# A fused two-block transformer kernel: where the squares of the recurrent heads' outputs are summed, and in what order VectorE gates and convolves

## Chip, cores and metric

The kernel runs on one core of one Trainium2 chip. The metric is the device time of one execution in microseconds (us); lower is better. The kernel before takes 2325.43 us, the median of three executions that lie between 2322.28 and 2327.88 us.

## The reference, cut to what matters

The reference is a diffusion-style block followed by a second block. The change touches only the second block's gated delta rule with eight heads of width 128 over 512 tokens, and there only what happens to its output `oa`:

```python
q = _l2norm(q) * 128 ** -0.5 ;  k = _l2norm(k)          # after a causal convolution of 4 taps and silu
for each chunk:   U = u_t - w @ S
                  o = q_dec @ S + p_intra @ U
                  S = S * exp(g_last) + k_dec.T @ U
oa = rmsnorm_2(oa, head_norm) * silu(za)                 # rmsnorm over the 128 columns of a head
y  = sigmoid(ga) * (oa @ w_a_out) + ...
```

`rmsnorm_2` needs, for each token and head, the sum of the squares of 128 values, then `1 / sqrt(sum / 128 + eps)`.

## The kernel before

The kernel is written engine by engine, with semaphores between the engines. Every large product is done three times over in single precision pieces: a weight block of 1 MB arrives in `raw`, ScalarE copies it to `w_hi` (line 742), GpSimd subtracts to get `w_lo` (line 670, four instructions for each block), and TensorE multiplies hi by hi, hi by lo and lo by hi (lines 2049 to 2051). These products keep TensorE busy nearly all the time.

The recurrent heads are worked in four pairs, `p` = 0 to 3, two heads (`a` = 0, 1) at a time. A pair needs four weight blocks (q, k, v, z). While TensorE does the small matrices of pair `p`, it fills its waits with pieces of the products for pair `p + 1` (`piece` and `fill`; a piece is six matmuls of 512 columns). 24 pieces, for q, k and v, go into the inversion levels and the four recurrence steps; the eight pieces of z stand behind them. The end of a pair, called the tail here, is this:

- ScalarE copies the output of each of the four steps `tt` from PSUM to `o_tok` (line 1164, 128x256). It then stores the v tiles of the next pair and splits a weight block (`pair_qkv(p + 1, 2)`, line 1176), waits for the sums, and takes the square root (line 1178).
- VectorE ends the convolutions 2 and 3 of the next pair (`convolve`, lines 1749 to 1756, four instructions for each), squares the whole of `o_tok` (line 1859), sums it (line 1860), waits for the root, inverts it (line 1862), scales `o_tok` in one instruction (line 1863), does convolution 4, then the two gatings (line 1869, `oaT`), then convolution 5.
- TensorE does pieces 0 to 3 of z, waits for the scaled `o_tok` (line 2616), transposes it (eight `turn`s, line 2158), does pieces 4 and 5, waits for the gated `oaT` (line 2624) and begins pair `p + 1`.
- The next pair begins with ScalarE's silu of convolutions 0 to 3, the squares of two of them (line 1117), silu of 4 and 5, then the roots (line 776). TensorE sums the squares with one-column matmuls (`sum_of`, line 2131), and between the first sums it has pieces 6 and 7 of z. Then it spreads the inverted roots over the partitions (`spread`, line 2152). The order is: sum 0, piece 6, sum 1, piece 7, spread 0, sum 2, spread 1, sum 3, spread 2, spread 3. ScalarE's queue puts the root of sum 0 behind silu 5, and silu 5 waits for convolution 5. Each spread is followed by a normalisation on VectorE, and behind the last ones come the transposes of k and v and the small products of the next pair, with no large product in between until `fill(3)` (line 2546).

In the last pair (`p` = 3) there is no next pair: TensorE does a whole gate block of sixteen pieces ahead of line 2616, and VectorE has no convolutions.

ScalarE's functions lie in tables; the program has a table load wherever the next function is not in the one that is loaded.

Of the kernel before, what the change touches and what calls it, by code (L numbers as in the profile page):

```python
# [19 lines left out]
ACT = mybir.ActivationFunctionType  # L20
ALU = mybir.AluOpType
AX = mybir.AxisListType


P = 128
# [3 lines left out]
NT = S // P  # L29
# [65 lines left out]
def build(nc, t, out):  # L95
# [23 lines left out]
    one_eps = fixed("one_eps", [P, 8])  # L119
# [4 lines left out]
    o_stat = fixed("o_stat", [P, 3, 8])  # L124
    sq2 = fixed("sq2", [P, 2, S])
    acc = fixed("acc", [P, S])
    tmp2 = fixed("tmp2", [P, 2, S])
# [107 lines left out]
    o_tok = r.over("o_tok", [P, 2, NT, P], decay_at)  # L235
# [53 lines left out]
    ps = nc.alloc_psum_tensor("ps", [P, 8, 512], F32)  # L289
# [12 lines left out]
    def over_width(m, w=P):  # L302

        return m.unsqueeze(2).broadcast_to([m.shape[0], m.shape[1], w])
# [123 lines left out]
    lat_std kr_mm kr_copied kr_put qk_scaled v_scaled qk_summed qk_squared qk_turned qk_stored qk_std at_turned at_exp  # L428
    at_copied at_out_hi fm_mm fm_hi_done y_t_done y_hi_done rsq_done g_hi_done gate_dve gate_act c_pad c_conv
    o_done c_silued c_sq Gb_mm Gb_exp d_diff d_exp nL_turned nLT_done lv_m1 lv_copied uw_mm uw_copied r_su r_oc  # L430
    o_sq o_std oa_hi_done m_tr m_T_done s_hi_done x_last y_turned dve_chain n_inv n_bc n_lo vec_tr tr_done
    ada_mod lat_gained lat_inv qk_mm qk_normed scl2_done at_scores at_prob at_out_lo fc_mm fc_half fc_split fz_done fm_lo_done
    y_lo_done g_lo_done ab_turned gate_cum c_normed kv_turned k_scaled qd_done kk_mm nL_done inv0_done lv_mm
    lv_done r_o r_ws r_u r_st o_scaled o_turned oa_lo_done rb_done gate_silu gate_scaled s_lo_done""".split()
    sem = {n: nc.alloc_semaphore(n) for n in names}
# [121 lines left out]
    with nc.Block() as block:  # L557
# [171 lines left out]
        def _(act):  # L729
# [118 lines left out]
            for j in range(2):  # L848
# [8 lines left out]
                                 scale=1.0 / KV_LORA).then_inc(sem["lat_std"], 1)  # L857
# [241 lines left out]
            for p in range(4):  # L1099
                u = first[f"pair{p}"]  # L1100
                if p == 0:
                    act.wait_ge(sem["c_pad"], 1)
                    pair_qkv(p, 0)
                    act.wait_ge(sem["gate_dve"], 3)
                    nc.scalar.activation(gp[:, 10, :, :], gp[:, 5, :, :], ACT.Exp)
                    nc.scalar.activation(gp[:, 8, :, :], gp[:, 9, :, :], ACT.Exp).then_inc(sem["gate_act"], 1)
                    pair_qkv(p, 1)
                    pair_qkv(p, 2)

                def silu(j):  # L1110
                    act.wait_ge(sem["c_conv"], 6 * p + j + 1)
                    nc.scalar.activation(conv[:, j, :], conv[:, j, :], ACT.Silu).then_inc(sem["c_silued"], 1)

                def square(j):
                    act.wait_ge(sem["c_silued"], 6 * p + j + 1)
                    act.wait_ge(sem["n_sum"], 4 + 4 * p + j - 1)
                    nc.scalar.activation(sq2[:, j % 2, :], conv[:, j, :], ACT.Square).then_inc(sem["c_sq"], 1)

                for j in range(4):
                    silu(j)  # L1120
                square(0)
                square(1)
                silu(4)
                silu(5)
                std_of(4 + 4 * p, 1.0)
                square(2)
                std_of(5 + 4 * p, 1.0)
                square(3)
                std_of(6 + 4 * p, 1.0)
                std_of(7 + 4 * p, 1.0)  # L1130
                for a in range(2):
                    if p:
                        act.wait_ge(sem["o_done"], 2 * p)
                    store_tile(u + 3, a, z_s[:, a, :], ACT.Silu)
                next_hi()
                for a in range(2):
                    h = 2 * p + a
                    act.wait_ge(sem["Gb_mm"], h + 1)
                    nc.scalar.activation(eGb[:, a, :], ps[:, 4 + a, :], ACT.Exp).then_inc(sem["Gb_exp"], 1)
                    act.wait_ge(sem["d_diff"], h + 1)  # L1140
                    nc.scalar.activation(decay[:, a, :, :], decay[:, a, :, :], ACT.Exp, scale=-1.0).then_inc(sem["d_exp"], 1)
                for a in range(2):
                    for i, dst in enumerate((nLT, prT)):
                        act.wait_ge(sem["nL_turned"], 4 * p + 2 * a + i + 1)
                        nc.scalar.activation(dst[:, a, :, :].rearrange("p t c -> p (t c)"), ps[:, (6 if i == 0 else 4) + a, :],
                                             ACT.Copy).then_inc(sem["nLT_done"], 1)
                for s in range(1, LEVELS):
                    for a in range(2):
                        n = (p * (LEVELS - 1) + s - 1) * 2 + a
                        act.wait_ge(sem["lv_m1"], n + 1)  # L1150
                        nc.scalar.activation(prod[:, a, :, :].rearrange("p t c -> p (t c)"), ps[:, 6 + a, :],  # L1151
                                             ACT.Copy).then_inc(sem["lv_copied"], 1)
                for a in range(2):
                    for i, dst in enumerate((u0[:, a, :, :].rearrange("p t c -> p (t c)"), wT[:, a, :])):
                        act.wait_ge(sem["uw_mm"], 4 * p + 2 * a + i + 1)
                        nc.scalar.activation(dst, ps[:, 4 + 2 * i + a, :], ACT.Copy).then_inc(sem["uw_copied"], 1)
                if p < 3:
                    pair_qkv(p + 1, 0)
                else:
                    gate_a(0)  # L1160
                    next_hi()
                for tt in range(NT):
                    act.wait_ge(sem["r_o"], 4 * p + tt + 1)
                    nc.scalar.activation(o_tok[:, :, tt, :], ps[:, 5 + 2 * (tt % 2), 0:2 * P].rearrange("p (a c) -> p a c", a=2),
                                         ACT.Copy).then_inc(sem["r_oc"], 1)
                    if tt == 1 and p < 3:
                        pair_qkv(p + 1, 1)
                    elif tt == 2 and p == 3:
                        gate_a(1)
                        next_hi()  # L1170
                    elif p == 3 and tt in (0, 1):
                        act.wait_ge(sem["o_done"], 6)
                        for k in range(3 * tt, 3 * tt + 3):
                            nc.scalar.activation(oa_hi[:, k, :], oaT[:, k, :], ACT.Copy).then_inc(sem["oa_hi_done"], 1)
                if p < 3:
                    pair_qkv(p + 1, 2)
                act.wait_ge(sem["o_sq"], p + 1)
                nc.scalar.activation(o_stat[:, 1, :], o_stat[:, 0, :], ACT.Sqrt, bias=one_eps[:, 0:1],
                                     scale=1.0 / P).then_inc(sem["o_std"], 1)


            for k in range(6, HA):
# [159 lines left out]
        def _(dve):  # L1342
            chain = [0]

            def link(ins):

                ins.then_inc(sem["dve_chain"], 1)
                chain[0] += 1
                dve.wait_ge(sem["dve_chain"], chain[0])

            V = nc.vector
# [87 lines left out]
            for i in range(2):  # L1439
                ins = V.scalar_tensor_tensor(scl[:, i, :], mod[:, 8:16, i], 1.0,  # L1440
                                             vecT[:, VEC_AT["norm1_g"]:VEC_AT["norm1_g"] + KT], ALU.add, ALU.mult)
# [173 lines left out]
            for j in range(4):  # L1615
                u, v, o = first["gf"] + j, merged("ga", j), merged("wfa", j)
                for jj in range(2):
                    dve.wait_ge(bank_stored[bank_of(u, jj)], stored_count(u, jj))
                    dve.wait_ge(sem["tile_done"], tile_count(o, jj))
                    p = bank(o, jj)  # L1620
# [4 lines left out]
                for jj in range(2):  # L1625
# [3 lines left out]
                    p = bank(o, 2 + jj)  # L1629
# [129 lines left out]
            def convolve(p, j):  # L1759
                convolve_a(p, j)  # L1760
                convolve_b(p, j)

            for p in range(4):
# [89 lines left out]
                    convolve(p + 1, 2)  # L1853
                    convolve(p + 1, 3)

                dve.wait_ge(sem["r_oc"], 4 * p + 4)
                flat = o_tok[:, :, :, :].rearrange("p a t c -> p (a t) c")
                sq = tmp2[:, :, :].rearrange("p a (t c) -> p (a t) c", c=P)
                link(V.tensor_tensor(sq, flat, flat, ALU.mult))
                V.tensor_reduce(o_stat[:, 0, :], sq, AX.X, ALU.add).then_inc(sem["o_sq"], 1)  # L1860
                dve.wait_ge(sem["o_std"], p + 1)
                link(V.reciprocal(o_stat[:, 2, :], o_stat[:, 1, :]))
                V.tensor_tensor(flat, flat, over_width(o_stat[:, 2, :]), ALU.mult).then_inc(sem["o_scaled"], 1)
                if p < 3:
                    convolve(p + 1, 4)
                for a in range(2):
                    dve.wait_ge(sem["o_turned"], 2 * p + a + 1)
                    dve.wait_ge(bank_stored[bank_of(u + 3, a)], stored_count(u + 3, a))
                    V.scalar_tensor_tensor(oaT[:, 2 * p + a, :], ps[:, 4 + a, :], col("head_norm_2"), z_s[:, a, :],
                                           ALU.mult, ALU.mult).then_inc(sem["o_done"], 1)  # L1870
                if p < 3:
                    convolve(p + 1, 5)

            for k in range(HA):
# [4 lines left out]
            for j in range(4):  # L1879
                u, v = gated("aout", "sig", j), gated("aout", "proj", j)  # L1880
                for jj in range(2):
                    dve.wait_ge(bank_stored[bank_of(u, jj)], stored_count(u, jj))
                    dve.wait_ge(sem["tile_done"], tile_count(v, jj))
                    p = bank(v, jj)
# [158 lines left out]
        def _(pe):  # L2043
# [448 lines left out]
            for p in range(4):  # L2492
# [120 lines left out]
                        piece(first[f"pair{p + 1}"] + 3, k)  # L2613
                else:
                    wide_gemm(gated("aout", "sig", 2), h_hi, h_lo)
                pe.wait_ge(sem["o_scaled"], p + 1)
                for a in range(2):
                    for tt in range(NT):
                        ins = turn(ps[:, 4 + a, tok(tt)], o_tok[:, a, tt, :])
                    ins.then_inc(sem["o_turned"], 1)  # L2620
# [224 lines left out]
```

## Time and profile before

| | before |
|---|---|
| median of three executions | 2325.43 us |
| the profiled execution | 2328.51 us |
| its span, first to last instruction | 2326.6 us |
| TensorE matmul busy | 2240.3 us (96%) |
| VectorE busy | 893.2 us (38%) |
| ScalarE busy | 830.4 us (36%) |
| GpSimd busy | 882.5 us (38%) |
| mean granted TensorE clock | 0.982 of full |

Times inside the span are microseconds from its start. A row of a timeline shows the start, the time that the merged instructions cover, the engine, the line, what is written and read, the count, and in brackets the time that the engine had been idle and what ended that. The three tails of pairs 0, 1 and 2 begin their transposes at 1015, 1124 and 1237 us, the tail of pair 3 at 1344 us. Matmuls overlap each other, so their durations add up to more than the time they take.

### The profile page before, as it was taken

To read this page: it belongs to the slowest core of one execution; us is meant where nothing else is said; L and a number is where in the kernel's file an instruction comes from. 1 tells how busy PE (TensorE), PEld (TensorE's weight loads), DVE (VectorE), ACT (ScalarE), POOL (GpSimd) and SP (SyncE) were. 2 spreads that over 40 slices of the span, in tenths; PEclk is the share of its full clock that TensorE was granted. 3 is DMA by queue.
4 is the path that set the end of the run, shared out by engine and by line. 5 is a ranking of instruction groups with operands and counts; after the bars stand their busy time and mean duration, and the time that the engine had idled before them with its cause. 6 is when DMAs were issued, how large, how long until landed. Compare 5 with 4: busy or idle time off the path is not lost.

```text
span 2326.6 us, 29170 instructions
## 1 busy us (share of the span) xinstructions
PE 2240.3 (96%) x11780; PEld 1862.3 (80%) x11780; DVE 893.2 (38%) x1411; ACT 830.4 (36%) x1208; POOL 882.5 (38%) x640
## 2 busy tenths in 40 slices
PE   6999999989999989989999999999999999999998
PEld 3767778878888868979797988888888988888887
DVE  2456855441211246474747320414143344222102
ACT  2455533232322335242424322535333443322212
POOL 0325953434444434030212144222254524444442
PEclk9989999999999999999999999999999999999998
DMA  6411333522233233020201022121232412322321
GB/s 229 149 54 55 127 102 103 169 73 91 91 96 102 91 110 96 19 73 9 101 19 55 19 91 92 54 94 52 100 118 91 135 50 90 107 90 94 104 90 55
DMA packets 179970, 205.93 MB, mean 89 GB/s; under 512 B 3364, under 2 KB 170768, under 8 KB 179472
## 3 DMA queue, kind: packets, MB, share of 16 engines
q1 hardware_dynamic: 176912, 195.17, 25.9%
q10 hardware_dynamic: 2944, 9.15, 1.1%
q8 instruction: 82, 1.34, 0.2%
q14 instruction: 32, 0.26, 0.0%
HBM read 198.01 MB, written 6.29 MB: 88 GB/s over the span
## 4 chain that ended last, share of the span: by engine, by line
PE 83%; DVE 6%; ACT 2%; POOL 2%; issue 1%; DMA 1%; ACTq 0%; DVEq 0%; SPq 0%
PE ps L2049 20%; PE ps L2051 20%; PE ps L2050 19%; PE ps L2158 3%; PE ps L2574 2%; PE ps L2565 2%; PE ps L2370 2%; POOL w_lo L670 2%; PE ps L2643 2%; PE ps L2572 2%; PE ps L2660 1%; PE ps L2152 1%; PE ps L2336 1%; PE ps L2096 1%; PE ps L2098 1%; PE ps L2097 1%
## 5 line engine op out<-in xcount | busy, mean ns | idle before, releaser
L670 POOL TENSOR_TENSOR w_lo<-raw,w_hi 128x512 fp32r<-128x512 f32 x586 | 780.3, 1363 | 1378.5 <-ACT w_hi L742 1378.5
L2049 PE MATMUL ps<-h_hi,w_hi 128*128 128x512 f32 x1384 | 560.4, 405 | 12.9 <-DVE h_lo L1389 4.2
L2051 PE MATMUL ps<-h_hi,w_lo 128*128 128x512 f32 x1384 | 544.3, 393 | 0.0
L2050 PE MATMUL ps<-h_lo,w_hi 128*128 128x512 f32 x1384 | 543.3, 393 | 0.0
L742 ACT ACTIVATE w_hi<-raw 128x2048 fp32r<-128x2048 f32 x150 | 285.7, 1905 | 373.5 <-PE ps L2051 365.7
L2049 PEld LDWEIGHTS ps<-h_hi,w_hi 128*128 128x128 f32 x1384 | 262.7, 190 | 74.1 <-issue 10.7
L2051 PEld LDWEIGHTS ps<-h_hi,w_lo 128*128 128x128 f32 x1384 | 262.4, 190 | 57.0
L2050 PEld LDWEIGHTS ps<-h_lo,w_hi 128*128 128x128 f32 x1384 | 263.0, 190 | 52.6 <-issue 1.5
L2049 PE MATMUL ps<-g_hi,w_hi 128*128 128x512 f32 x256 | 101.0, 394 | 0.0
L2051 PE MATMUL ps<-g_hi,w_lo 128*128 128x512 f32 x256 | 100.4, 392 | 0.0
L2050 PE MATMUL ps<-g_lo,w_hi 128*128 128x512 f32 x256 | 99.4, 388 | 0.0
L1656 DVE SCALAR_TENSOR_TENSOR xT<-ps,mod,xT 128x512 f32<-128x512 f32 x40 | 30.0, 751 | 167.2 <-PE ps L2051 167.1
L1900 DVE SCALAR_TENSOR_TENSOR score_b<-ps,xT 128x128 f32<-128x128 f32 (+3 forms) x64 | 31.3, 490 | 152.0 <-PE ps L2643 145.6
L1151 ACT ACTIVATE prod<-ps 128x512 f32<-128x512 f32 x48 | 28.7, 598 | 129.6 <-PE ps L2565 129.6
L1693 DVE TENSOR_TENSOR rsq<-relu 128x512 f32<-128x512 f32 x32 | 22.2, 693 | 133.1 <-ACT relu L761 133.1
L2049 PE MATMUL ps<-s_hi,w_hi 128*128 (+1 forms) x176 | 69.4, 394 | 1.0 <-issue 1.0
L2051 PE MATMUL ps<-s_hi,w_lo 128*128 (+1 forms) x176 | 69.0, 392 | 0.0
L2050 PE MATMUL ps<-s_lo,w_hi 128*128 (+1 forms) x176 | 68.3, 388 | 0.0
L1830 DVE COPY_PREDICATED inv<-masks,ps 128x512 f32<-128x512 uint32 x40 | 29.2, 730 | 83.2 <-PE ps L2574 83.2
L761 ACT ACTIVATE relu<-ps 128x512 f32<-128x512 f32 x32 | 19.1, 598 | 108.3 <-PE ps L2051 102.6
L2051 PEld LDWEIGHTS ps<-g_hi,w_lo 128*128 128x128 f32 x256 | 48.1, 188 | 11.3
L2050 PEld LDWEIGHTS ps<-g_lo,w_hi 128*128 128x128 f32 x256 | 48.1, 188 | 10.7
(414 smaller groups left out, 3939.5 us busy)
## 6 DMA issues: line engine op xcount, KB each, us to landing
raw<-w_in SPq DMA_DIRECT2D x48, 1024.0 KB, 5.2
raw<-w_down SPq DMA_DIRECT2D x27, 1024.0 KB, 5.1
raw<-ada_w SPq DMA_DIRECT2D x24, 1024.0 KB, 5.2
raw<-w_gate_up SPq DMA_DIRECT2D x22, 1024.0 KB, 5.1
raw<-w_up SPq DMA_DIRECT2D x16, 1024.0 KB, 5.4
raw<-w_mkv SPq DMA_DIRECT2D x8, 1024.0 KB, 5.5
raw<-w_out SPq DMA_DIRECT2D x4, 1024.0 KB, 5.5
xT<-bias_band SPq DMA_DIRECT2D x2, 2048.0 KB, 9.9
```

The lines of the kernel that those rows point to most:

```text
L670: ins = nc.gpsimd.tensor_tensor(w_lo[:, split_at[u] % 2, cols], raw[:, u % 2, cols], w_hi[:, split_at[u] % 2, cols].bitcast(F32), ALU.subt ...
L742: nc.scalar.activation(w_hi[:, split_at[u] % 2, 0:n], raw[:, u % 2, 0:n], ACT.Copy).then_inc(sem["w_hi_done"], 1)
L1900: V.scalar_tensor_tensor(score_b[:, n % 3, 0:nk], ps[:, 2 + n % 2, 0:nk], -(DB ** -0.5), xT[:, hh, S - nk:S], ALU.mult, ALU.subtract).then ...
L2049: T.matmul(out_, wh, hi, start=start, stop=False, skip_group_check=True)
L2050: T.matmul(out_, wh, lo, start=False, stop=False, skip_group_check=True)
L2051: return T.matmul(out_, wl, hi, start=False, stop=stop, skip_group_check=True)
L2158: return T.transpose(out_, src, const[0:rows, CONST_AT["ident"]:CONST_AT["ident"] + rows])
L2370: ins = T.matmul(ps[(h % 2) * 64:(h % 2 + 1) * 64, out_bank(n), tok], v[:, kt, (h % 8) * 64:(h % 8 + 1) * 64], pT[:, n % 2, kt * P:(kt + 1 ...
L2565: ins = T.matmul(ps[:, 6 + a, tok(tt)], nLT[:, a, tt, :], inv[:, a, tt, :], start=True, stop=True)
L2572: T.matmul(ps[:, 4 + a, tok(tt)], invT[:, a, tt, :], prod[:, a, tt, :], start=True, stop=True)
L2574: ins = T.matmul(ps[:, 6 + a, tok(tt)], prod[:, a, tt, :], invT[:, a, tt, :], start=True, stop=True)
L2643: T.matmul(ps[:, 2 + n % 2, 0:nk], query[:, tok(q)], kbT[:, hh // 2, 0:nk], start=True, stop=True).then_inc(sem["b_scores"], 1)
```

## The change

The two large instructions of VectorE that square and sum `o_tok` go. Instead ScalarE, right after each of its copies out of PSUM, runs two `Square` activations over the same PSUM values (128x128 each, one for each head) and has each leave its row sum in a column of `o_stat`. The root is taken at once behind the fourth step, ahead of the stores and the split in `pair_qkv(p + 1, 2)`. VectorE scales `o_tok` in two halves, one for each head, with a count of the semaphore for each, and TensorE waits for each half by itself. VectorE's gatings move in front of convolution 4, so that both convolutions 4 and 5 stand behind them.

```diff
@@ ScalarE
                 for tt in range(NT):
                     act.wait_ge(sem["r_o"], 4 * p + tt + 1)
-                    nc.scalar.activation(o_tok[:, :, tt, :], ps[:, 5 + 2 * (tt % 2), 0:2 * P].rearrange("p (a c) -> p a c", a=2),
-                                         ACT.Copy).then_inc(sem["r_oc"], 1)
+                    out_of = ps[:, 5 + 2 * (tt % 2), 0:2 * P].rearrange("p (a c) -> p a c", a=2)
+                    nc.scalar.activation(o_tok[:, :, tt, :], out_of, ACT.Copy)
+                    for a in range(2):
+                        ins = nc.scalar.activation(tmp2[:, a, tt * P:(tt + 1) * P], out_of[:, a, :], ACT.Square,
+                                                   accum_out=o_stat[:, 0, a * NT + tt:a * NT + tt + 1])
+                    ins.then_inc(sem["r_oc"], 1)
...
+                act.wait_ge(sem["r_oc"], 4 * p + 4)
+                nc.scalar.activation(o_stat[:, 1, :], o_stat[:, 0, :], ACT.Sqrt, bias=one_eps[:, 0:1],
+                                     scale=1.0 / P).then_inc(sem["o_std"], 1)
                 if p < 3:
                     pair_qkv(p + 1, 2)
-                act.wait_ge(sem["o_sq"], p + 1)
-                nc.scalar.activation(o_stat[:, 1, :], o_stat[:, 0, :], ACT.Sqrt, bias=one_eps[:, 0:1],
-                                     scale=1.0 / P).then_inc(sem["o_std"], 1)
@@ VectorE
-                dve.wait_ge(sem["r_oc"], 4 * p + 4)
-                flat = o_tok[:, :, :, :].rearrange("p a t c -> p (a t) c")
-                sq = tmp2[:, :, :].rearrange("p a (t c) -> p (a t) c", c=P)
-                link(V.tensor_tensor(sq, flat, flat, ALU.mult))
-                V.tensor_reduce(o_stat[:, 0, :], sq, AX.X, ALU.add).then_inc(sem["o_sq"], 1)
                 dve.wait_ge(sem["o_std"], p + 1)
                 link(V.reciprocal(o_stat[:, 2, :], o_stat[:, 1, :]))
-                V.tensor_tensor(flat, flat, over_width(o_stat[:, 2, :]), ALU.mult).then_inc(sem["o_scaled"], 1)
-                if p < 3:
-                    convolve(p + 1, 4)
+                for a in range(2):
+                    V.tensor_tensor(o_tok[:, a, :, :], o_tok[:, a, :, :], over_width(o_stat[:, 2, a * NT:(a + 1) * NT]),
+                                    ALU.mult).then_inc(sem["o_scaled"], 1)
                 for a in range(2):
                     dve.wait_ge(sem["o_turned"], 2 * p + a + 1)
                     dve.wait_ge(bank_stored[bank_of(u + 3, a)], stored_count(u + 3, a))
                     V.scalar_tensor_tensor(oaT[:, 2 * p + a, :], ps[:, 4 + a, :], col("head_norm_2"), z_s[:, a, :],
                                            ALU.mult, ALU.mult).then_inc(sem["o_done"], 1)
                 if p < 3:
+                    convolve(p + 1, 4)
                     convolve(p + 1, 5)
@@ TensorE
-                pe.wait_ge(sem["o_scaled"], p + 1)
                 for a in range(2):
+                    pe.wait_ge(sem["o_scaled"], 2 * p + a + 1)
                     for tt in range(NT):
                         ins = turn(ps[:, 4 + a, tok(tt)], o_tok[:, a, tt, :])
                     ins.then_inc(sem["o_turned"], 1)
```

The semaphore `o_sq` goes with them.

## Rows read from the trace of the kernel before

**Rows 1.** The page's chain that ended last, shares of the span by engine.
```profile
PE 83%; DVE 6%; ACT 2%; POOL 2%; issue 1%; DMA 1%; ACTq 0%; DVEq 0%; SPq 0%
```
**Rows 2.** Who waited for whom, first tail (1012 to 1035): total, times, longest.
```profile
PE ps L2131 <- DVE oaT L1869: 2.2, 1, 2.2
...
PE ps L2158 <- DVE o_tok L1863: 1.5, 1, 1.5
```
**Rows 3.** Table by stretch: length, TensorE busy (matmuls), granted clock, DMA share, GB/s.
```profile
1015.00:1021.00 6.00, 3.84 (x20) 1.00 0.35 105
...
1132.00:1136.00 4.00, 4.00 (x15) 0.50 0.00 0
...
1248.00:1252.00 4.00, 4.00 (x14) 0.50 0.00 0
```
**Rows 4.** Timeline of TensorE, tails of pairs 0, 1 and 2.
```profile
1015.12 1.09 PE L2158 MATMUL ps<-const,o_tok 128*128 128x128 f32 x8 [1.49 <-DVE o_tok L1863]
...
1021.15 1.05 PE L2131 MATMUL ps<-const,sq 128*128 128x1 f32 x8 [2.19 <-DVE oaT L1869]
...
1026.44 1.13 PE L2152 MATMUL ps<-const,stat 128*128 128x128 f32 x8 [0.49 <-DVE stat L1369]
...
1123.88 1.09 PE L2158 MATMUL ps<-const,o_tok 128*128 128x128 f32 x8 [1.49 <-DVE o_tok L1863]
...
1129.91 1.75 PE L2131 MATMUL ps<-const,sq 128*128 128x1 f32 x8 [2.19 <-DVE oaT L1869]
...
1138.50 1.91 PE L2152 MATMUL ps<-const,stat 128*128 128x128 f32 x8
...
1236.75 1.09 PE L2158 MATMUL ps<-const,o_tok 128*128 128x128 f32 x8 [1.49 <-DVE o_tok L1863]
```
**Rows 5.** Timeline of VectorE in the first tail.
```profile
1010.37 1.22 DVE L1859 TENSOR_TENSOR tmp<-o_tok 128x1024 f32<-128x1024 f32 x1
...
1013.45 1.61 DVE L1863 TENSOR_TENSOR o_tok<-o_tok,o_stat 128x1024 f32<-128x1024 f32 x1
1014.98 1.50 DVE L1749 TENSOR_SCALAR conv<-pad_in,vecT 128x512 f32<-128x512 f32 x1
1016.51 1.68 DVE L1750 SCALAR_TENSOR_TENSOR conv<-pad_in,vecT,conv 128x512 f32<-128x512 f32 x1
...
1019.69 1.40 DVE L1869 SCALAR_TENSOR_TENSOR oaT<-ps,vecT,z_s 128x512 f32<-128x512 f32 x2
...
1023.09 0.75 DVE L1756 SCALAR_TENSOR_TENSOR conv<-pad_in,vecT,conv 128x512 f32<-128x512 f32 x1
```
**Rows 6.** Timeline of ScalarE in the first tail.
```profile
1008.17 0.39 ACT L1164 ACTIVATE o_tok<-ps 128x256 f32<-128x256 f32 x1 [6.50 <-PE ps L2608]
...
1009.41 1.93 ACT L742 ACTIVATE w_hi<-raw 128x2048 fp32r<-128x2048 f32 x1
...
1013.20 1.28 ACT L1112 ACT_TABLE_LOAD   x1
1014.49 2.20 ACT L1112 ACTIVATE conv<-conv 128x512 f32<-128x512 f32 x4
1016.59 1.14 ACT L1117 ACTIVATE sq<-conv 128x512 f32<-128x512 f32 x2
```
**Rows 7.** ScalarE's groups by shape, whole span: busy us, mean ns of one.
```profile
L1221 ACT ACTIVATION_READ_ACCUMULATOR prob_b<-score_b,b_min 128x1 f32 x64 | 12.3, 192 | 0.0
...
L1229 ACT ACTIVATE probT_b<-ps 128x128 f32<-128x128 f32 x16 | 4.4, 277 | 19.5 <-PE ps L2158 19.5
```
**Rows 8.** Timeline of GpSimd in the first tail.
```profile
1011.42 6.23 POOL L670 TENSOR_TENSOR w_lo<-raw,w_hi 128x512 fp32r<-128x512 f32 x4 [8.08 <-ACT w_hi L742]
```
**Rows 9.** Timeline of VectorE in the last pair's tail.
```profile
1338.50 1.62 DVE L1863 TENSOR_TENSOR o_tok<-o_tok,o_stat 128x1024 f32<-128x1024 f32 x1
```
**Rows 10.** Timeline of TensorE in the last pair's tail.
```profile
1343.95 1.03 PE L2158 MATMUL ps<-const,o_tok 128*128 128x128 f32 x8
```
**Rows 11.** Table by stretch around 311 us, columns as in rows 3.
```profile
311.00:316.00 5.00, 5.00 (x40) 0.83 0.69 209
```

More of the change, by code:

```diff
@@ L430, in build @@
     o_done c_silued c_sq Gb_mm Gb_exp d_diff d_exp nL_turned nLT_done lv_m1 lv_copied uw_mm uw_copied r_su r_oc
-    o_sq o_std oa_hi_done m_tr m_T_done s_hi_done x_last y_turned dve_chain n_inv n_bc n_lo vec_tr tr_done
+    o_std oa_hi_done m_tr m_T_done s_hi_done x_last y_turned dve_chain n_inv n_bc n_lo vec_tr tr_done
     ada_mod lat_gained lat_inv qk_mm qk_normed scl2_done at_scores at_prob at_out_lo fc_mm fc_half fc_split fz_done fm_lo_done
```

## The prediction

> **What bounds the kernel now.** I read the page's chain first: 83% of it is TensorE [rows 1]. So VectorE's or ScalarE's time counts only where TensorE waits for it. Then the waits of one tail: TensorE waits 1.5 us for the scaled `o_tok` and 2.2 us for `oaT` [rows 2]. Last the granted clock by stretch: 1.00 in the first tail, and 0.50, the 1.2 GHz level, in the other two [rows 3], behind the same two waits [rows 4]. The timelines then give the order of work. All times below are in the first tail's own time; the other tails are the same, shifted by 108.8 and 221.6 us.
>
> TensorE's idle times in the first tail: 1.49 ahead of the transposes at 1015.12, 2.19 ahead of sum 0 at 1021.15, 0.49 ahead of spread 0 at 1026.44, together 4.17 us [rows 4]. The fallen clock is dearer. From 1123.88 to 1236.75 are 112.87 us, from 1015.12 to 1123.88 are 108.76 [rows 4]: the fall behind the second tail costs 4.11 us, and one more fall stands behind the third. The profiled execution has two, 8.2 us. Without them its 2328.51 us would be 2320.3. It lies 3.1 us above the median 2325.43, about the price of one fall less.
>
> **VectorE's part.** The squares and sums took 2.5 us ahead of the root (start 1010.37) [rows 5]. They go. What VectorE waits for now is ScalarE: the fourth copy starts at 1008.17 and takes 0.39 [rows 6]. Two Squares with an accumulator read each are added. No row has a Square of that shape with a sum; the nearest are the 128x128 copy out of PSUM at 0.277 and the accumulator read at 0.192 [rows 7]. Overlapped completely a pair costs ScalarE 0.55, one behind the other 0.94; I take 0.75, nearer the middle. Root: table load 1.28 (the length that a load has in rows 6), root 0.30, so it is there at 8.56 + 0.75 + 1.6 = 1010.9 (10.7 to 11.1). The inversion adds 0.25. Half a scaling is no row; half of 1.61 is 0.81, half of the plain 1.22 is 0.61 [rows 5]. I take 0.75. Both halves are ready at about 1012.7. TensorE's four pieces end at 15.12 - 1.49 = 1013.6 [rows 4]. The **first wait goes**, 1.5 us, and the two halves gain nothing more, because both are early.
>
> The earlier twelve pairs of Squares lie in waits of ScalarE, which was idle 6.50 us ahead of the fourth copy [rows 6]; they cost nothing. If one were late by its 0.75, the steps' fills would still cover it.
>
> The transposes now start at 1013.6. Gating a takes the half transposed, 0.6 later, and the pair of gatings takes 1.4 [rows 5]: 1014.2 to 1015.6. TensorE has pieces 4 and 5: from the transposes' start to their end it was 21.15 - 2.19 - 15.12 = 3.84 us [rows 4], so they end at 1017.45. The **second wait**, for `oaT`, **goes** too.
>
> **What is late next.** Sum 0 needs a square of a silu on ScalarE. Its queue: root till 1010.9, stores and split 2.9 (from the copy's end at 8.56, less the overlap, to the split's end at 11.34), load 1.28, four silus 2.1, one square 0.6: 1017.8. Sum 0 starts at 1017.9, 3.2 us earlier than now, after 0.4 us of waiting.
>
> From there TensorE has 26.44 - 0.49 - 21.15 = 4.80 us of work [rows 4], till 1022.7. Spread 0 hangs on something else: on convolution 5, through silu 5, a table load, the root and the inversion. That convolution ended at 1023.84 [rows 5], spread 0 began at 1026.44 [rows 4]: 2.60 us behind it. Where does it end now? Gatings till 1015.6, then both convolutions. One that nothing disturbs took 23.84 - 21.01 = 2.83 us [rows 5], counted from its first instruction, which overlaps the gatings by 0.08. But GpSimd's four subtractions follow the split. They began at 1011.42 and covered 6.23 us [rows 8]. Now the split stands behind the root and ends at 1013.8, so they run until about 1020. VectorE's instructions beside them are longer: the first two of convolution 4 took 1.50 and 1.68, while one of the second's kind alone takes 0.75, and convolution 4 took 19.69 - 14.98 = 4.71 [rows 5], 1.9 us more than 2.83, for two such instructions. Now it lies wholly beside GpSimd: three of its instructions would be caught, +2.8. Bounds: two caught, +1.9; four, +3.7. Convolution 5 ends at 15.6 + 2 x 2.83 + 2.8 = 1024.0 (23.1 to 24.9), against 1023.84. The 2.5 us saved on VectorE go into 1.5 us of waiting for the transposes and 0.9 us more beside GpSimd.
>
> So spread 0 starts at 1026.6 (25.7 to 27.5), where it started at 1026.44. **The sum without the clock** is nothing: +0.2 us a tail (-0.7 to +1.1). The idle time is 0.4 + 3.9 = 4.3, where it was 4.17. But it lies in one piece of 3.9 us (3.0 to 4.8) instead of pieces of 1.5, 2.2 and 0.5.
>
> **The last pair** has slack: its scaling began at 1338.50 and took 1.62 [rows 9], and the transposes came at 1343.95 [rows 10], 3.8 us later. ScalarE's steps there are about 0.75 later each, which the gate block covers. Zero; if that cover were gone, at most 1 us.
>
> **The clock.** It fell in two of three tails after idles of 1.49 and 2.19 with 3.84 us of pieces between [rows 3, 4]. It also fell at 311 to 316 us with TensorE never idle, in a run of one-column sums [rows 11]. Now the idle is 3.9 us, longer than any in these tails, with one-column sums around it. And behind it stand spreads and sums only, no pieces. I expect a fall in each of the three tails. A spread group took 1.91 at the low level against 1.13, a sum 1.75 against 1.05 [rows 4]. Four spreads and two sums on the path: 4 x 0.78 + 2 x 0.70 = 4.5. The first transposes behind them add some 0.7 (estimate, half a group of the 1.03 of rows 10 more). A fall costs 5.2 us. Low end 3.0, if it comes one spread and one sum late and has gone before the transposes; high end 8, if it lasts into the small products, where both engines take turns until `fill(3)`.
>
> The Trainium skill (TensorE: Matmul & The Clock Gate, section Why this matters for your kernels) asks that bursts of matmuls have no long idle gap between them, lest the clock fall. That speaks against joining the waits.
>
> The Trainium skill (ScalarE: Activation LUTs, section What ACT_TABLE_LOAD costs) adds 1.38 us of drain to each 1.28 us load. By that, two loads ahead of sum 0 would put it at 1020.7; its 4.80 us of work still end ahead of spread 0, and the sum stays. The row speaks against it: the load that starts at 1013.20 is followed by the silu at 1014.49 [rows 6].
>
> **How it adds up.** 2328.5 - 8.2 (two falls that the old waits caused) + 3 x 0.2 + 3 x 5.2 = 2336.5 us. Where convolution 4 meets only two subtractions it is 2.7 less. I forecast 2335.
>
> **Rivals.**
> - *The clock holds.* The stalls move and no fall comes: 2320.3 + 0.6 = 2321; with the shorter convolution 4, 2318. For it: the first tail had 4.2 us of idle and no fall. Against: never one piece of this length in a tail. It decides if convolution 5 ends so early that the idle ahead of spread 0 stays near the 2.19 that the first tail bore. The price is three falls of 5.2, 15.6 us. Chance 0.20.
> - *Some falls only, or cheap ones.* Two falls of 5.2, 2331, or three of 3.0, 2330, down to one, 2326. For it: one tail in three was spared before. Chance 0.22.
> - *The clock stays low until the next large product.* Mechanism: behind spread 0 come only short matmuls until `fill(3)`, and if these do not bring the clock back, all TensorE's steps in the chain stay doubled. 2321 + 3 x 8 = 2345. It decides if the transposes of k and v still run at the low level. Chance 0.08.
> - *The change does not do what it says*, by Square needing a table of its own: one load of 1.28 more in each pair, hidden in ScalarE's waits before the first step. It changes nothing and is within the above.
> - My forecast, three falls of about 5: 2329 to 2340, chance 0.50. It is the case that ends slower.
>
> **How the numbers follow.** 0.2% of the median is 4.7 us, about what a measurement of this kernel can tell from no change. Faster is below 2320.8: most of the first rival and a little more, 0.20. Slower is above 2330.1: the forecast but its lowest part, a quarter of the second rival, all of the third, 0.56. Same: 0.24. For eight in ten the range takes in both other sides: 2317 to 2343. That leaves out part of the third rival and the lowest ends. The forecast's own range is 2329 to 2340.
>
> **What would show it.** Right: no wait of TensorE for `o_tok` or `oaT` in the three tails; transposes some 13 us in front of spread 0 (11.3 now), one idle of 3 to 4.8 us ahead of spread 0; convolution 4 with three long instructions; clock 0.50 over the spreads of each tail; VectorE's busy time down by 4 x 2.5, less what GpSimd adds, ScalarE's up by 16 x 0.75 to 0.94. Wrong: an idle under 2.5 us ahead of spread 0 (the convolution's price was too high), a clock of 1.00 behind a long idle (then the time is near 2320), or a wait ahead of sum 0 of over 1.5 us (ScalarE's queue was mis-sized).

## The result and the profile after

The changed kernel takes 2332.03 us, the median of eight runs (2327.89 to 2338.45); the kernel before takes 2323.94 us beside it (eight runs, 2320.61 to 2327.88). The ratio is 1.0033, 95% interval 1.0023 to 1.0043: slower by a third of a percent. The profiled execution of the changed kernel took 2330.06 us, its span is 2328.3 us.

| | before | after |
|---|---|---|
| TensorE matmul busy, us | 2240.3 | 2243.0 |
| VectorE busy, us | 893.2 | 880.5 |
| ScalarE busy, us | 830.4 | 838.6 |
| mean granted clock | 0.982 | 0.981 |
| from the first tail's transposes to the second's | 108.76 | 114.40 |
| from the second's to the third's | 112.87 | 113.07 |

The chain is still TensorE's, 84% where it was 83% [rows 1]. Here is TensorE's timeline of the changed kernel in the first tail (start, time covered, line, count, and in brackets the idle time before and what ended it). The rest of such a tail are pieces of six matmuls.

```profile
1008.04 1.03 PE L2158 MATMUL ps<-const,o_tok 128*128 128x128 f32 x8
...
1012.17 1.02 PE L2131 MATMUL ps<-const,sq 128*128 128x1 f32 x8 [0.34 <-issue]
...
1014.53 0.95 PE L2131 MATMUL ps<-const,sq 128*128 128x1 f32 x8
...
1020.48 2.04 PE L2152 MATMUL ps<-const,stat 128*128 128x128 f32 x8 [3.49 <-DVE stat L1373]
1022.32 1.71 PE L2131 MATMUL ps<-const,sq 128*128 128x1 f32 x8
1023.88 2.05 PE L2152 MATMUL ps<-const,stat 128*128 128x128 f32 x8
1025.73 1.71 PE L2131 MATMUL ps<-const,sq 128*128 128x1 f32 x8
1027.30 3.76 PE L2152 MATMUL ps<-const,stat 128*128 128x128 f32 x16
1031.84 3.67 PE L2158 MATMUL ps<-const,conv 128*128 128x128 f32 x16 [0.78 <-DVE conv L1780]
```

Against rows 4: the transposes follow the pieces with no wait (1.49 us before), sum 0 waits 0.34 us (2.19 before), and spread 0 waits 3.49 us (0.49 before). From there on a spread group covers 2.04 us against 1.13 [rows 4]. The other two tails have the same three idle times within 0.03 us.

The same kernel's table by stretch (length, busy time and count of TensorE, weight loads, VectorE, ScalarE, GpSimd, then granted clock, DMA share, GB/s):

```profile
1012.00:1016.00 4.00, 3.83 (x25) 3.50 (x26) 3.89 (x5) 1.22 (x3) 1.79 (x2) 1.00 0.24 57
1016.00:1020.00 4.00, 0.99 (x5) 0.47 (x3) 1.81 (x3) 2.05 (x3) 0.00 (x0) 0.88 0.58 206
1020.00:1024.00 4.00, 3.52 (x17) 3.55 (x17) 1.04 (x3) 1.31 (x4) 0.00 (x0) 0.50 0.00 0
...
1032.00:1036.00 4.00, 4.00 (x20) 4.00 (x21) 2.56 (x5) 1.23 (x1) 3.99 (x4) 0.50 0.01 2
1136.00:1140.00 4.00, 4.00 (x21) 4.00 (x21) 0.87 (x2) 0.26 (x1) 0.00 (x0) 0.50 0.00 0
1248.00:1252.00 4.00, 4.00 (x19) 4.00 (x20) 1.05 (x3) 1.04 (x4) 0.00 (x0) 0.50 0.00 0
```

The clock falls around the end of the idle ahead of spread 0, in all three tails: in stretches of half a microsecond the fall begins 1.5 us ahead of spread 0 in the first tail, 0.2 us behind its start in the second and 0.2 us ahead of it in the third. Before, the first tail kept 1.00 and the others fell behind their second wait [rows 3]. VectorE's timeline of the changed kernel in the first tail, answering to rows 5:

```profile
1005.29 0.20 DVE L1861 RECIPROCAL o_stat<-o_stat 128x8 f32<-128x8 f32 x1 [0.27 <-ACT o_stat L1180]
1005.53 1.29 DVE L1863 TENSOR_TENSOR o_tok<-o_tok,o_stat 128x512 f32<-128x512 f32 x2
1008.68 1.41 DVE L1868 SCALAR_TENSOR_TENSOR oaT<-ps,vecT,z_s 128x512 f32<-128x512 f32 x2 [1.85 <-PE ps L2158]
1010.00 0.94 DVE L1753 TENSOR_SCALAR conv<-pad_in,vecT 128x512 f32<-128x512 f32 x1
1010.98 1.67 DVE L1754 SCALAR_TENSOR_TENSOR conv<-pad_in,vecT,conv 128x512 f32<-128x512 f32 x1
1012.68 1.66 DVE L1759 SCALAR_TENSOR_TENSOR conv<-pad_in,vecT,conv 128x512 f32<-128x512 f32 x1
...
1017.13 0.75 DVE L1760 SCALAR_TENSOR_TENSOR conv<-pad_in,vecT,conv 128x512 f32<-128x512 f32 x1
```

The scaling is ready 1.2 us ahead of the transposes, VectorE then waits 1.85 us for them, and three instructions of convolution 4 are long. GpSimd in the same stretch:

```profile
1008.12 5.67 POOL L670 TENSOR_TENSOR w_lo<-raw,w_hi 128x512 fp32r<-128x512 f32 x4 [9.77 <-ACT w_hi L742]
```

ScalarE's timeline shows what the Squares cost, which no row of before had:

```profile
1002.75 0.39 ACT L1165 ACTIVATE o_tok<-ps 128x256 f32<-128x256 f32 x1 [5.98 <-PE ps L2608]
1003.03 0.27 ACT L1167 ACTIVATE tmp<-ps 128x128 f32<-128x128 f32 x1
1003.18 0.21 ACT L1167 ACTIVATION_READ_ACCUMULATOR tmp<-ps 128x1 f32 x1
1003.28 0.28 ACT L1167 ACTIVATE tmp<-ps 128x128 f32<-128x128 f32 x1
1003.43 0.21 ACT L1167 ACTIVATION_READ_ACCUMULATOR tmp<-ps 128x1 f32 x1
1003.67 1.28 ACT L1180 ACT_TABLE_LOAD   x1
1004.96 0.30 ACT L1180 ACTIVATE o_stat<-o_stat,one_eps 128x8 f32<-128x8 f32 x1
```

A pair of Squares with their reads ends 0.50 us behind the copy's end (1003.64 against 1003.14).

The two profiled spans differ by only 1.7 us, though the three tails together lost 6.2 us (from the end of the first tail's pieces to the last pair's transposes 336.50 us, before 330.32). The rest was gained where nothing was changed: the first tail's pieces end 5.6 us earlier in the execution of after (1008.0 against 1013.6). Ahead of them the granted clock fell six times, and seven times in the execution of before, where several falls were also longer. A single execution is a draw of such falls, and medians are needed.

### The profile page after: what moved, and what is told of

Same layout as the page of the kernel before. It is cut to its first block, busy times and chain, and to the rows that moved or that the text cites. A ratio compares the mean times of both kernels' runs of the same rounds, so it can differ in the third digit from the quotient of the medians.

```text
span 2328.3 us, 29230 instructions
## 1 busy us (share of the span) xinstructions
PE 2243.0 (96%) x11780; PEld 1869.0 (80%) x11780; DVE 880.5 (38%) x1407; ACT 838.6 (36%) x1272; POOL 878.6 (38%) x640
## 4 chain that ended last, share of the span: by engine, by line
PE 84%; DVE 5%; ACT 2%; POOL 2%; issue 1%; DMA 1%; ACTq 0%; DVEq 0%; SPq 0%
PE ps L2049 20%; PE ps L2051 20%; PE ps L2050 20%; PE ps L2158 3%; PE ps L2574 2%; PE ps L2565 2%; PE ps L2370 2%; POOL w_lo L670 2%; PE ps L2643 2%; PE ps L2572 2%; PE ps L2152 1%; PE ps L2660 1%; PE ps L2336 1%; PE ps L2096 1%; PE ps L2098 1%
## 5 line engine op out<-in xcount | busy, mean ns | idle before, releaser
L2050 PEld LDWEIGHTS ps<-g_lo,w_hi 128*128 128x128 f32 x256 | 48.1, 188 | 10.7
```

The costliest lines, as they stand in the source:

```text
L2050: T.matmul(out_, wh, lo, start=False, stop=False, skip_group_check=True)
```

## The experiments

Theory A is that of the prediction: the steps themselves come out even, convolution 5 sets spread 0 and joins the idle times into one, and the clock falls there. The rivals are in the expectations. All experiments ran beside the kernel before; where the first four ran its median was 2325.38, where the last four ran 2324.00 us. So a time of one group and a time of the other can be told apart only to about 1.4 us. The ratios are as recorded; for the first four they lie about 0.001 above the quotient of the two medians given here.

**One edit of the order undone.** Convolution 4 stands ahead of the gatings again.

```diff
+                if p < 3:
+                    convolve(p + 1, 4)
                 for a in range(2):
                     dve.wait_ge(sem["o_turned"], 2 * p + a + 1)
...
                 if p < 3:
-                    convolve(p + 1, 4)
                     convolve(p + 1, 5)
```

> The changed kernel with one edit undone: convolution 4 stands again between the scaling and the gatings. Theory A (the long idle ahead of spread 0 lets the clock fall, and it comes from both convolutions standing behind the gatings, beside GpSimd): here convolution 4 runs from 1012.7 on, in the time in which VectorE now waits for the transposes, and partly ahead of GpSimd's subtractions; convolution 5 ends 1.5 to 2.5 us earlier in each tail than in the changed kernel, spread 0 comes at most 2.5 us after the last piece, few or no falls stand behind the three tails: 2312 to 2318 us, 0.6 to 0.9% under the changed kernel and faster than the kernel before. Rival B (ScalarE's Squares and reads are what costs): nothing changes, 2330 to 2334 us, and the clock falls as in the changed kernel.

Measured: 2325.78 us (2319.23 to 2332.19), ratio 1.0012, interval 1.0000 to 1.0025. Neither number of the expectations came: the kernel is no faster than the kernel before. TensorE in the three tails of that kernel:

```profile
1011.96 1.02 PE L2132 MATMUL ps<-const,sq 128*128 128x1 f32 x8 [0.35 <-DVE oaT L1870]
...
1018.82 1.88 PE L2153 MATMUL ps<-const,stat 128*128 128x128 f32 x8 [2.09 <-DVE stat L1373]
...
1130.80 1.28 PE L2153 MATMUL ps<-const,stat 128*128 128x128 f32 x8 [2.11 <-DVE stat L1373]
...
1242.84 1.13 PE L2153 MATMUL ps<-const,stat 128*128 128x128 f32 x8 [2.08 <-DVE stat L1373]
```

The steps behave as theory A has it: the idle ahead of spread 0 is 2.1 us, 1.4 less. But the clock still fell in all three tails of the profiled execution (0.50 over 1020 to 1028, 1132 to 1144 and 1248 to 1256 us). My belief that an idle of 2 us would be borne was wrong. Rival B is refuted too: the kernel is 6 us faster than the changed one with every Square in place.

**The other edit alone.** The kernel before, with the gatings ahead of both convolutions.

```diff
-                if p < 3:
-                    convolve(p + 1, 4)
                 for a in range(2):
                     dve.wait_ge(sem["o_turned"], 2 * p + a + 1)
...
                 if p < 3:
+                    convolve(p + 1, 4)
                     convolve(p + 1, 5)
```

> The kernel before with one edit of the change alone: VectorE's gatings in front of convolutions 4 and 5, everything else as before. Theory A: the first wait of 1.49 us stays, the second (2.19 us) goes, since the gatings end about 1.7 us ahead of TensorE's piece 5; the idle ahead of spread 0 grows from 0.49 to about 2.5 us, because convolution 5 ends where it did (1023.8 in the first tail's time). Falls in one to three of the tails: 2322 to 2334 us. Rival B (the Squares on ScalarE are what costs): no different from the kernel before or up to 2 us faster, whatever the idle ahead of spread 0.

Measured: 2326.09 us (2322.56 to 2334.23), ratio 1.0010, interval 0.9999 to 1.0021, inside theory A's range. Rival B's number (no different from the kernel before) is met as well, so this time alone does not tell them apart; the trace has the steps that theory A named. The idle ahead of spread 0 is 1.99 us, the second wait is gone. In the profiled execution the clock held in the first tail and fell in the other two. With the fall a tail's period is 113.05 us, without it 107.79, against 108.76 before. So this order saves 1.0 us in the steps and loses it in falls.

**The subtractions moved away.** The changed kernel, with the tail's split between silu 4 and silu 5 of the next pair.

```diff
-            def pair_qkv(p, kind):
+            def pair_qkv(p, kind, split=True):
...
                     store_tile(first[f"pair{p}"] + kind, a, pad_in[:, 2 * kind + a, 3:3 + S])
-                next_hi()
+                if split:
+                    next_hi()
...
                 silu(4)
+                if p:
+                    next_hi()
                 silu(5)
...
                 if p < 3:
-                    pair_qkv(p + 1, 2)
+                    pair_qkv(p + 1, 2, split=False)
```

> The changed kernel with one wait's cause moved: ScalarE's split of a weight block that follows the stores in the tail (and with it GpSimd's four subtractions) stands between silu 4 and silu 5 of the next pair instead, about 8 us later. Theory A: convolutions 4 and 5 have no subtraction beside them, take 2 x 2.83 instead of about 8, convolution 5 ends 2 to 2.8 us earlier, the idle ahead of spread 0 is 1 to 1.6 us instead of 3.5, the clock holds in all three tails: 2311 to 2316 us. Rival C (the convolutions' length does not matter, spread 0 waits for ScalarE's queue): the split delays silu 5 and the root by up to 1.9 us, spread 0 comes later than in the changed kernel, 2332 us or more.

Measured: 2315.78 us (2309.39 to 2324.6), ratio 0.9967, interval 0.9954 to 0.9980. The convolutions are now short, here VectorE in the first tail:

```profile
1011.68 0.48 DVE L1756 TENSOR_SCALAR conv<-pad_in,vecT 128x512 f32<-128x512 f32 x1
1012.19 0.75 DVE L1757 SCALAR_TENSOR_TENSOR conv<-pad_in,vecT,conv 128x512 f32<-128x512 f32 x1
1012.98 0.75 DVE L1762 SCALAR_TENSOR_TENSOR conv<-pad_in,vecT,conv 128x512 f32<-128x512 f32 x1
...
1016.52 0.75 DVE L1763 SCALAR_TENSOR_TENSOR conv<-pad_in,vecT,conv 128x512 f32<-128x512 f32 x1
```

Both take 5.59 us (from 1011.68 to 1017.27) instead of 7.88 in the changed kernel (from 1010.00 to 1017.88). That settles the price of the subtractions beside them: 2.3 us a tail. Rival C is refuted. The idle ahead of spread 0 is 1.86 us, more than the 1 to 1.6 us expected. In the profiled execution no tail had a fall. But that execution is the fastest of the twelve, 6.4 us under the median, and its mean granted clock is 0.989, while the median of the twelve is 0.985. So most of the others had falls that this trace does not show; whether they stood in these tails, no trace tells. That the time came out inside theory A's range is therefore no proof that the clock held.

**TensorE kept busy in the idle of the changed kernel.** Twelve matmuls that nobody reads stand behind piece 7.

```diff
+                def keep_busy(n):
+                    for _ in range(n):
+                        T.matmul(ps[:, 7, :], h_hi[:, 0, 0:P], h_hi[:, 0, :], start=True, stop=True)
...
                         piece(u + 3, 6 + j)
+                    if p and j == 1:
+                        keep_busy(12)
```

> The changed kernel with twelve matmuls of 512 columns added behind piece 7 in each of the three tails, into a bank of PSUM that nobody reads; they do no work of the reference and take about 2.7 us at the full clock, inside the idle of 3.5 us. Theory A (the loss is the clock, and the idle makes it fall): spread 0 starts no later than before, the clock stays at 1.00 over the spreads and transposes, each tail is 4 to 6 us shorter, 2315 to 2320 us. Rival D (the clock falls because of the spreads and one-column sums themselves, or the tail is longer for another reason): falls stay, 2330 to 2336 us.

Measured: 2314.15 us (2312.25 to 2319.89), ratio 0.9965, interval 0.9951 to 0.9979. This is 17.9 us under the changed kernel, with more work and nothing taken away, and 0.9 us below theory A's range. TensorE in its first tail, and the table by stretch:

```profile
1022.66 1.13 PE L2152 MATMUL ps<-const,stat 128*128 128x128 f32 x8 [0.83 <-DVE stat L1373]
...
1029.04 1.97 PE L2158 MATMUL ps<-const,conv 128*128 128x128 f32 x16 [0.78 <-DVE conv L1780]
```

```profile
1018.00:1022.00 4.00, 3.84 (x17) 2.83 (x16) 1.99 (x3) 1.88 (x2) 0.00 (x0) 1.00 0.63 220
1022.00:1026.00 4.00, 3.33 (x30) 3.37 (x31) 1.60 (x5) 1.75 (x6) 0.00 (x0) 1.00 0.00 0
```

Spread 0 comes 12.42 us behind the transposes (1022.66 - 1010.24), in the changed kernel 12.44. What differs is the clock and what follows at it: from spread 0 to the first matmul of `fill(3)` are 15.58, 15.23 and 15.23 us here, 21.39, 20.05 and 19.99 in the changed kernel. Rival D is refuted in these tails: spreads and sums alone did not bring the clock down.

**TensorE kept busy in the waits of the kernel before.**

```diff
+                if p < 3:
+                    keep_busy(6)
                 pe.wait_ge(sem["o_scaled"], p + 1)
...
+                    keep_busy(9)
                     pe.wait_ge(sem["o_done"], 2 * p + 2)
```

> The kernel before with matmuls of 512 columns added into the two waits of each of the three tails, six ahead of the wait for the scaled outputs and nine ahead of the wait for the gated ones, into a bank of PSUM that nobody reads; they do no work of the reference. Theory A (a fall of the clock stands behind the waits of some tails of the kernel before, two in the profiled execution): none is left there, each spared fall gives back 4 us: 2316 to 2322 us, under the kernel before by one to one and a half falls on the mean, with less spread. Rival (the falls behind these tails are not made by these waits): 2323 to 2328 us, as the kernel before.

Measured: 2315.61 us (2313.19 to 2320.42), ratio 0.9964, interval 0.9950 to 0.9977, 8.4 us under the kernel before, 0.4 us below theory A's range. Its periods are 108.78 us in both cases. So the kernel before loses 8.4 us to falls behind its old waits. At 4.1 us each that is two on the mean, not one to one and a half. Kept busy, before and after differ by 1.5 us (2315.61 and 2314.15, whose runs overlap). In the traces the changed kernel's two periods are shorter by 0.2 and 0.6 us (108.58 and 108.21 from transposes to transposes). So the change's steps come out about even.

**Both improvements together.** Convolution 4 ahead of the gatings as in the first experiment, and the late split of the third; the diffs are those two.

> The changed kernel with both edits of the first runs: convolution 4 in front of the gatings again, and ScalarE's split between silu 4 and silu 5. Theory A: convolution 4 runs in VectorE's wait for the transposes, nothing stands beside it on GpSimd, convolution 5 ends some 4.5 us earlier than in the changed kernel, spread 0 finds its root ready when piece 7 ends; no idle of over 0.5 us in a tail, no fall there: 2303 to 2309 us, 0.7 to 0.9% under the kernel before. Rival (the late split moves the wait to silu 5 and GpSimd's subtractions into the gatings or the normalisation): an idle of 1 us or more ahead of spread 0 or later, 2311 us or more, no better than the late split alone.

Measured: 2304.26 us (2300.69 to 2306.78), ratio 0.9915, interval 0.9898 to 0.9931, as theory A had it. TensorE in its first tail has no idle from the transposes to the ones of k and v:

```profile
1009.94 1.03 PE L2162 MATMUL ps<-const,o_tok 128*128 128x128 f32 x8
...
1013.56 0.95 PE L2135 MATMUL ps<-const,sq 128*128 128x1 f32 x8
...
1018.16 1.13 PE L2156 MATMUL ps<-const,stat 128*128 128x128 f32 x8
...
1024.54 1.97 PE L2162 MATMUL ps<-const,conv 128*128 128x128 f32 x16 [0.78 <-DVE conv L1783]
```

The 0.78 us ahead of the transposes of k and v, over the 0.5 us of theory A, are in all the kernels here. The root for spread 0 is inverted at 1018.02, as piece 7 ends, so the rival's wait there did not come. The periods are 104.38 and 104.02 us, 4.4 and 8.9 below the two of before. This kernel beats both, before and after.

**One scaling instead of two halves.**

```diff
-                for a in range(2):
-                    V.tensor_tensor(o_tok[:, a, :, :], o_tok[:, a, :, :], over_width(o_stat[:, 2, a * NT:(a + 1) * NT]),
-                                    ALU.mult).then_inc(sem["o_scaled"], 1)
+                flat = o_tok[:, :, :, :].rearrange("p a t c -> p (a t) c")
+                V.tensor_tensor(flat, flat, over_width(o_stat[:, 2, :]), ALU.mult).then_inc(sem["o_scaled"], 1)
```

> The changed kernel with the scaling done in one instruction and one count again, as in the kernel before; all else is the changed kernel. Theory A (the halves gain nothing, since the scaled outputs are ready about 1.2 us before TensorE's pieces end): within 2 us of the changed kernel, 2330 to 2334 us, the transposes start without a wait. Rival (the halves are what takes away the first wait): a wait of 0.3 us or more ahead of the transposes comes back.

Measured: 2333.13 us (2330.13 to 2336.81), ratio 1.0039, interval 1.0027 to 1.0052, 1.1 us from the changed kernel, with no wait ahead of the transposes. The halves gain nothing.

**The first experiment, kept busy.** Its kernel with `keep_busy(8)` behind piece 7.

> The changed kernel with convolution 4 in front of the gatings again, and eight matmuls of 512 columns behind piece 7 in each of the three tails, into a bank of PSUM that nobody reads; they do no work of the reference and take 1.8 us of the idle of 2.1 us. Theory A (that order gains 1.8 us a tail in the steps, and the falls behind an idle of 2.1 us took it back): no fall in the tails, 1.6 to 1.9 us a tail under the changed kernel that was kept busy: 2307 to 2312 us. Rival (the falls come for another reason): 2322 to 2328 us, as without these matmuls.

Measured: 2313.93 us (2309.07 to 2318.74), ratio 0.9956, interval 0.9943 to 0.9969. The falls in the tails are gone and with them 11.9 us against the kernel that was not kept busy. From sum 0 to sum 0 its tails are 107.17 and 106.81 us apart, against 108.58 and 108.21 in the changed kernel kept busy, so the steps are 1.4 us a tail shorter; from the first tail's transposes to the last pair's they are 4.2 us shorter (316.84 against 321.09). The medians do not show it: 0.2 us instead of 4.2, and above the 2307 to 2312 that theory A wanted. In the profiled execution the clock fell once more ahead of the first tail than in that of the changed kernel kept busy (at 136 to 148 us; both fell at about 916), and once more behind the tails (1628 to 1636). The other runs point the same way: the median of their mean granted clocks is 0.987, against 0.988 to 0.989 there, and among runs whose mean clock is 0.989 the three there took 2312.25 to 2313.97 us, the two here 2309.07 and 2310.35, 3.6 us less on the mean. So at an equal clock most of the gain is there, and further falls hide it; why this kernel has more of them, and where they lie in the other runs, stays open.

## Why the prediction was right, point by point

The forecast was 2335 us and slower, by three falls of the clock behind one long idle. It was 2332.03. The direction and the mechanism came as told. That the number lies within 3 us is in part luck. The sum stood on 2320.3 us for the kernel before without its two falls, taken from one profiled execution that lies 4.6 us above the median of the eight; kept busy, that kernel takes 2315.61, 4.7 us less. Against that, the new falls came out dearer (17.9 us by the medians instead of 15.6) and the steps cheaper (-1.5 instead of +0.6). The difference between the two kernels is the fairer test: the sum makes it -8.2 + 0.6 + 15.6 = 8.0 us, and it is 8.1.

To compare steps, 5.56 us are added to the times of after, so that the pieces end at 1013.6 in both.

- *Both waits go*: right. The root was ready at 1010.8 (forecast 1010.9), both halves at 1012.4 (1012.7), the gatings ran from 1014.2 to 1015.65 (1014.2 to 1015.6).
- *A pair of Squares costs 0.75 us*: too high, it is 0.50; ScalarE's busy time rose by 8.2 us, 0.51 for each pair, not 12 to 15. Of the 0.21 us of a read 0.12 lie inside its Square. It moved nothing, since the scaling was early anyway.
- *Sum 0 after 0.4 us of waiting at 1017.9*: 0.34 us, 1017.7.
- *Convolutions 4 and 5 take 8.4 us beside the subtractions*: 7.9. Three instructions were caught, as forecast, but the first by only 0.46 us. The late split measured this price by itself.
- *Spread 0 at 1026.6 behind one idle of 3.9 us*: 1026.0 and 3.5 us, inside the bounds.
- *The sum without the clock is nothing*: forecast +0.2 us a tail. The changed kernel kept busy is 1.5 us under the kernel before kept busy, so about -0.5 us a tail (-0.2 and -0.6 by the periods of the traces).
- *The old waits cost two falls, 8.2 us*: 8.4 by keeping the kernel before busy.
- *Three falls of 5.2 us*: in the traces 5.8, 4.8 and 4.8 us between spread 0 and `fill(3)`, mean 5.1; by the medians 17.9 us for the three, 6.0 each. What makes the medians' number the larger is not settled; a few falls elsewhere would do it, since the changed kernel's median lies 2.0 us above its profiled execution.
- *VectorE's busy time down by four times 2.5 us, less what GpSimd adds*: it fell by 12.7 us, more than forecast. The eight squares and sums of the kernel before had held 10.7; the rest was not followed up.
- *The 1.38 us of drain that go with a table load by the Trainium skill* (ScalarE: Activation LUTs, section What ACT_TABLE_LOAD costs): the measurement decides against it here. The read ahead of the load ends at 1003.64, the load runs from 1003.67 to 1004.95, and the root starts at 1004.96, so there is no room for it on either side.
- *The rule that bursts of matmuls should have no long idle between them* (the Trainium skill, TensorE: Matmul & The Clock Gate, section Why this matters for your kernels): the traces agree, with the clock at 0.50 behind the idle of 3.49 us, and behind shorter ones of 1.99 to 2.19 us as well.

One belief that was not in the sum failed: in the rival where the clock holds, and in the first experiment's expectation, I took an idle near 2.1 us as borne. It had been in one tail of three. In the profiled executions it was borne in none of three tails (2.1 us, convolution 4 ahead of the gatings), in one of three (1.99, the other edit alone) and in three of three (1.86, the late split), the last in the fastest of twelve runs. So no length of idle that is safe here has been shown. What kept the clock at 1.00 in all three tails, with medians that bear it out, was to fill the idle or to have none ahead of spread 0 (both improvements together, which has no added matmuls).

## What to carry to other kernels

When a change takes away two short waits of the busiest engine, work out where its next wait ends. If it waits for the same last instruction of another engine, the idle is not gone but gathered, and a gathered idle can cost more through the clock than the short ones did. Put the freed engine's work into its own new wait (here convolution 4, while the transposes are made), and look at what GpSimd does beside VectorE's instructions with two inputs in SBUF. Before judging such a change, fill the idle with matmuls that nobody reads: it shows in one run how much of the difference is clock.

## What the runs showed of the hardware

- A fall of the clock costs what follows it: 4.1 us where pieces followed [rows 4], 4.8 to 5.8 us where spreads, sums and transposes followed. In the first tail of after the clock was at the 1.2 GHz level until 1036.0 us, 15.6 us after spread 0 began, in the other two for about 10 us behind spread 0.
- A tensor-scalar instruction of VectorE takes 0.48 us alone and 0.61 to 1.50 beside GpSimd's subtractions, a scalar-tensor-tensor with both inputs in SBUF 0.75 and up to 1.68. The gatings, which read one input from PSUM, kept 1.41 us for two beside them. The scaling of 128x1024 took 1.61 beside them [rows 5] and 1.22 alone (one scaling).
- Two 128x128 Squares out of PSUM with their row sums cost ScalarE 0.50 us. The accumulator's read is recorded with 0.21 us, but the next Square starts 0.10 us behind the read's start, so a read adds about 0.1 us (an estimate; no run has these Squares without their sums).
